# Expert places ranked by token count: capacities of 128, 96 and 64 rows, and the last ten experts two at a time in the array

## The chip, the cores and the metric

The kernel runs on one core of one Trainium2 chip. The metric is the device time of one execution in microseconds, as the median over the runs shown. All data is float32.

## The reference

One step of a single-layer decoder over 1088 tokens (1024 of a prompt, 64 of eight samples). RMSNorm and one input projection feed an RWKV-7 head group and a dilated-attention head group; their outputs are projected and added to h. Then comes the mixture of experts, which this case is about, then a gated per-layer embedding and a last RMSNorm.

```python
x = RMSNorm(h)                                    # 1088 x 1024
lg = x @ rgw + rgb;  gsel = argmax(lg)            # one of 4 groups
le_sel = (x @ rew + reb)[gsel]                    # 8 experts of that group
top_p, top_i = top_k(softmax(le_sel), 2)          # two experts per token
gate[token, expert] = softmax(lg)[gsel] * top_p / sum(top_p)
hg = silu(x @ ewg[e]) * (x @ ewu[e])              # 32 experts, 1024 -> 256
h += sum_e (hg * gate[:, e]) @ ewd[e]             # 256 -> 1024
```

There are 32 experts and 1088 x 2 = 2176 (token, expert) choices.

## The kernel before, in words

`build` runs five stages one after another: `inputs`, `rwkv`, `attention`, `feed_forward`, `finish`. Between the last two stands `later_passes`, which is skipped when no expert has more than CAP = 128 tokens (L2171: `most > CAP`).

`feed_forward` first projects the mixer outputs, normalises, and computes router logits. VectorE picks each token's experts (L1935 to L1962). TensorE counts (`rank`, L1717). VectorE works out each token's place in its expert and a one-hot of the places (L1965 to L1968), and TensorE multiplies that with the token numbers (`find`, L1723), so that bank 7 holds, for every expert, the list of its tokens. VectorE casts it to `idx` (L1973), which releases GpSimd's gathers and SyncE's load of expert 3.

Then comes the loop over the 32 experts in their own order, each with 128 rows whatever its count. For expert e:

- GpSimd gathers 128 token rows of 1024 values (0.5 MB) from HBM into one of three buffers (L1652).
- TensorE turns them (`gather_turn`, L1737: 8 transposes), VectorE copies the result out as `xT` (L2019).
- TensorE computes gate and up (`up`, L1750): for each of 2 matrices, 2 halves of the 256 hidden columns and 8 blocks of the contraction, one matmul with 128x128 *weights* as the stationary operand and 128 tokens as the moving one, 32 in all. A float32 matmul stands in the profile as two records, so 64.
- ScalarE applies silu (L1859), VectorE multiplies by the up half (L2030), giving `hT`.
- TensorE computes the down projection (`down`, L1762): 4 matmuls with `hT` stationary and 512 moving columns, 8 records. ScalarE copies out (L1827) and stores 0.5 MB to `y_rows` (L1830).

TensorE's order is written out by hand (L1794 to L1801): up(e), gather_turn(e+1), down(e-1), then up(e+1). Weights (three DMAs of 1 MB per expert, `load_expert`, L1560 to L1564) go into a ring of NW = 4 slots, slot e % 4. SyncE issues the load of expert e only when down(e-4) is done, since that frees the slot (L1634 to L1636). After down(29) it loads the 4 MB of the embedding gate into slots 0 and 1 (L1639 to L1641).

VectorE also works out, in turns 1 and 2, the row and weight of every token's result (`rows`, L1985), 33 small operations each.

`finish` gathers each token's two result rows (L2209), adds them, normalises, and does the last projection with TensorE (L2271, L2286).

Of the kernel before, what the change touches and what calls it, by code (L numbers as in the profile page):

```python
# [1544 lines left out]
NW, NX = 4, 3  # L1545
WSIZE = 2 * KD * FF + 2 * D
# [19 lines left out]

def feed_forward(nc, g):
# [3 lines left out]
    with ExitStack() as ctx:  # L1571
# [12 lines left out]
        w4, w32, br = w3[:, at + 256:at + 256 + G], w3[:, at + 260:at + 260 + NE], w3[:, at + 292:at + 292 + G + NE]  # L1584

# [6 lines left out]
        gated = g.gated = sb("gated", [128, 2, 2, 2 * CAP])  # L1592
        sg_, hT = ([gated[:, a, i, :].rearrange("p (f q) -> p f q", f=2) for i in range(2)] for a in range(2))
# [6 lines left out]
        pos, t1, t2, over, mx, pg, dl, rstd, ffn = (g.spare[:, a:a + TT] for a in range(330, 330 + 9 * TT, TT))  # L1600
        m2 = g.spare[:, 420:420 + 2 * TT].rearrange("p (k t) -> p k t", k=2)
# [4 lines left out]
        valid, tokv = sb("valid", [128, TT]), sb("tokv", [128, TT])  # L1606
# [5 lines left out]
        LOADS = ((gain, g.d_ffn_gain), (wr, g.d_wr), (br, g.d_br), (upper, g.d_upper), (iota, g.d_iota), (valid[:, :], g.d_valid),  # L1612
                 (w4, g.d_w4), (w32, g.d_w32), (tokv[:, :], g.d_tokv), (i32t, g.d_i32t), (pad_a, g.d_pad_a))
        with nc.Block() as block:
            @block.sync
            def _(sp):
# [27 lines left out]
            def _(pool):  # L1644
# [4 lines left out]
                for e in range(NE):  # L1649
                    if e >= NX:  # L1650
                        pool.wait_ge(s["x_turned"], e - NX + 1)
                    pool.indirect_dma_start(xg[e % NX], None, g.xn[:, :], bass.IndirectOffsetOnAxis(idx[:, e:e + 1], 0)).then_inc(xg_in[e % NX], 16)  # L1652
# [3 lines left out]
            def _(pe):  # L1656
# [74 lines left out]
                def gather_turn(e):  # L1731
                    pe.wait_ge(xg_in[e % NX], 16 * (e // NX + 1))
                    if e >= 1:
                        pe.wait_ge(s["xev"], e)
                    v = xg[e % NX].rearrange("p (q k) -> p k q", k=KD)
                    for k in range(KD):
                        mm = pe.transpose(bank[4 + k // 4][:, 128 * (k % 4):128 * (k % 4) + 128], v[:, k, :], g.ident[:, :])  # L1737
                    mm.then_inc(s["x_turned"], 1)

                def up(e):  # L1740
                    i = e % NW
                    pe.wait_ge(s["xev"], e + 1)
                    pe.wait_ge(w_in[i], 48 * (e // NW + 1))
                    wg, wu, _ = weights[i]
                    if e >= 2:
                        pe.wait_ge(s["h"], e - 1)
                    for a, w in enumerate((wg, wu)):
                        for f in range(2):
                            for k in range(KD):
                                mm = pe.matmul(bank[6 + e % 2][:, 128 * (2 * a + f):128 * (2 * a + f) + CAP], w[:, k, 128 * f:128 * f + 128],  # L1750
                                               xT[e % 2][:, k, :], start=(k == 0), stop=(k == KD - 1))
                    mm.then_inc(s["up"], 1)

                def down(e):
                    pe.wait_ge(s["h"], e + 1)
                    if e >= 2:
                        pe.wait_ge(s["yev"], e - 1)
# [109 lines left out]
            def _(dve):  # L1867
                def op(ins):
                    dve.drain()
# [674 lines left out]
```

## Time and profile before

| | us |
|---|---|
| median of 3 runs (1776.92 to 1789.27) | 1778.75 |
| the profiled execution's own time | 1779.9 |
| its span, first to last instruction | 1778.1 |
| TensorE busy | 1628.3 (92%) |
| VectorE busy | 672.5 (38%) |
| ScalarE busy | 434.6 (24%) |
| expert loop, first up to end of last down | 1249.6 to 1617.6 |

The span is what the profile shows; the time around it is 1.8 us. PE is TensorE's matmul side, PEld its weight loads, DVE VectorE, ACT ScalarE, POOL GpSimd, SP SyncE; SPq marks instructions of SyncE's queue. PEclk is the granted TensorE clock as a share of 2.4 GHz.

### The profile page before, as it was taken

What the parts mean: (1) busy time and instruction counts of PE and PEld (TensorE: products, weight loads), DVE (VectorE), ACT (ScalarE), POOL (GpSimd) and SP (SyncE); (2) the same over time, 40 slices, a digit from 0 to 9 for tenths busy, and PEclk for the clock granted to TensorE, in tenths of its full rate; (3) what the DMA queues carried; (4) which work ended last, traced back from release to release, by engine and by line L of the source; (5) the groups of instructions that cost most, each with busy time, mean ns of one, the idle gap of its engine ahead of it and who ended that gap; (6) DMA issues with size and microseconds to landing.
All of it is one profiled execution on the core that took longest, in us unless ns stands there. A gap on an engine that the chain in (4) does not pass through costs nothing. (4 is left out here: it accounts for less than half of the span.)

```text
span 1778.1 us, 34951 instructions
## 1 busy us (share of the span) xinstructions
PE 1628.3 (92%) x15296; PEld 1144.4 (64%) x15296; DVE 672.5 (38%) x1631; ACT 434.6 (24%) x891; POOL 55.5 (3%) x57
## 2 busy tenths in 40 slices
PE   7899989989988889998989879999999999995997
PEld 4566775775676656675757654555788888883443
DVE  5365464464364213415151442234411111112564
ACT  4413314214202202304131231112111111111344
POOL 0000000000000000000000000000100000002110
PEclk9898999998997889999999989999999999997999
DMA  5000001000010043403242472004799999976321
GB/s 183 27 27 12 15 17 38 13 16 13 15 41 20 3 195 129 169 27 155 119 179 119 186 276 97 36 36 158 273 368 368 366 371 368 365 297 221 111 83 42
DMA packets 57597, 246.90 MB, mean 139 GB/s; under 512 B 7520, under 2 KB 18016, under 8 KB 47712
## 3 DMA queue, kind: packets, MB, share of 16 engines
q1 hardware_dynamic: 45632, 201.61, 30.3%
q0 software_dynamic: 7200, 26.22, 4.1%
q10 hardware_dynamic: 4608, 16.78, 2.3%
q8 instruction: 123, 2.02, 0.5%
q14 instruction: 34, 0.28, 0.1%
HBM read 210.70 MB, written 33.88 MB: 138 GB/s over the span
## 5 line engine op out<-in xcount | busy, mean ns | idle before, releaser
L438 PE MATMUL bank<-h,w 128*128 128x352 f32 (+1 forms) x576 | 198.6, 495 | 6.4 <-DVE xb L997 6.4
L1750 PEld LDWEIGHTS bank<-cache,we 128*128 128x128 f32 x1536 | 175.1, 192 | 13.7 <-issue 10.5
L1750 PE MATMUL bank<-cache,we 128*128 128x128 f32 x1536 | 175.6, 275 | 2.8 <-DVE cache L2019 2.8
L438 PEld LDWEIGHTS bank<-h,w 128*128 128x128 f32 x576 | 109.7, 198 | 69.6 <-DVE xb L997 7.6
L2019 DVE COPY cache<-bank 128x512 f32<-128x512 f32 x64 | 41.3, 686 | 289.3 <-PE bank L1737 289.3
L1241 PE MATMUL bank<-h,w 128*128 128x352 f32 (+1 forms) x384 | 120.8, 477 | 5.5 <-POOL qd L1226 5.5
L1681 PE MATMUL bank<-cache,mixed 128*128 128x512 f32 x256 | 113.0, 600 | 6.4 <-DMA mixed<-in_pad_a 6.4
L2286 PE MATMUL bank<-we,unT 128*128 128x512 f32 x256 | 114.2, 604 | 1.4 <-DVE unT L2237 1.4
L1241 PEld LDWEIGHTS bank<-h,w 128*128 128x128 f32 x384 | 74.2, 194 | 50.4 <-POOL qd L1226 6.1
L1681 PEld LDWEIGHTS bank<-cache,mixed 128*128 128x128 f32 x256 | 48.7, 193 | 65.5 <-issue 58.9
L2286 PEld LDWEIGHTS bank<-we,unT 128*128 128x128 f32 x256 | 48.9, 194 | 60.4 <-issue 58.6
L1762 PE MATMUL bank<-we,gated 128*128 128x512 f32 x192 | 86.4, 592 | 0.0
L1297 PE MATMUL bank<-ident,score 128*128 128x128 f32 x288 | 45.9, 294 | 26.5 <-ACT score L1416 14.1
L1257 PEld LDWEIGHTS bank<-w,h 128*128 128x128 f32 (+1 forms) x576 | 65.3, 186 | 2.6
L1257 PE MATMUL bank<-w,h 128*128 128x128 f32 (+1 forms) x576 | 66.0, 275 | 0.0
L1444 DVE TENSOR_TENSOR eT<-bank,sin 128x352 f32<-128x352 f32 (+1 forms) x24 | 12.8, 536 | 138.1 <-PE bank L1249 136.7
L1827 ACT ACTIVATE cache<-bank 128x512 f32<-128x512 f32 x64 | 34.7, 594 | 123.5 <-PE bank L1762 123.5
L1297 PEld LDWEIGHTS bank<-ident,score 128*128 128x128 f32 x288 | 32.3, 146 | 50.1 <-ACT score L1416 28.5
L1859 ACT ACTIVATE gated<-bank 128x256 f32<-128x256 f32 x32 | 12.3, 385 | 199.2 <-PE bank L1750 199.2
L1750 PEld LDWEIGHTS bank<-cache 128*128 128x128 f32 x512 | 58.4, 192 | 3.8 <-issue 3.8
L1480 DVE CUSTOM_DVE_ANT_0 score<-bank,count 128x512 f32<-128x512 f32 (+3 forms) x96 | 50.9, 555 | 26.4 <-PE bank L1286 26.4
L1750 PE MATMUL bank<-cache 128*128 128x128 f32 x512 | 58.5, 275 | 0.0
(405 smaller groups left out, 2499.2 us busy)
## 6 DMA issues: line engine op xcount, KB each, us to landing
we<-in_weg SPq DMA_DIRECT2D x24, 1024.0 KB, 5.3
we<-in_weu SPq DMA_DIRECT2D x24, 1024.0 KB, 8.6
we<-in_wed SPq DMA_DIRECT2D x24, 1024.0 KB, 11.2
cache<-in_kcj SPq DMA_DIRECT2D x4, 5120.0 KB, 15.7
cache<-in_vcj SPq DMA_DIRECT2D x4, 5120.0 KB, 15.1
y_rows<-cache ACTq DMA_DIRECT2D x32, 512.0 KB
cache<-in_weg SPq DMA_DIRECT2D x8, 1024.0 KB
cache<-in_weu SPq DMA_DIRECT2D x8, 1024.0 KB
```

The source lines that it names most:

```text
L438: mm = pe.matmul(out[:, 0:w], w3[:, KIND[q], kd, :], g.uT[:, kd, a:a + w], start=(kd == 0), stop=(kd == KD - 1))
L1241: mm = pe.matmul(bank[QK[i][n]][:, 0:w], w3[:, k, i, :], g.uT[:, k, a:a + w], start=(k == 0), stop=(k == KD - 1))
L1257: mm = pe.matmul(bank[2 + n % 2][0:rows, 128 * (t - t0):128 * (t - t0) + 128], g.uT[:, k, 128 * t:128 * t + rows], w3[:, k, 2, :], start=( ...
L1297: mm = pe.transpose(bank[x % 2][:, 128 * (b - b0):128 * (b - b0) + 128], score[:, i % 2, hh, 128 * b:128 * b + 128], g.ident[:, :])
L1444: dve.tensor_tensor(turned[:, a:a + w], bank[QK[i][n]][:, 0:w], sin[:, a:a + w], ALU.mult)
L1480: dve.tensor_tensor_reduce(out=score[:, i % 2, hh, 512 * b:512 * b + w], in0=bank[4 + 2 * hh + (b if i >= 4 else i % 2)][:, 0:w], in1=coun ...
L1681: mm = pe.matmul(bank[2 * part + i][:, :], rows[:, k, 128 * t:128 * t + 128], wo[:, J * part + k, 512 * i:512 * i + 512], start=(k == 0), ...
L1750: mm = pe.matmul(bank[6 + e % 2][:, 128 * (2 * a + f):128 * (2 * a + f) + CAP], w[:, k, 128 * f:128 * f + 128], xT[e % 2][:, k, :], start= ...
L1762: mm = pe.matmul(bank[2 * (e % 2) + c][:, :], hT[e % 2][:, f, :], weights[e % NW][2][:, f, 512 * c:512 * c + 512], start=(f == 0), stop=(f ...
L1827: last = act.activation(yo[:, e % 2, 512 * c:512 * c + 512], bank[2 * (e % 2) + c][:, :], ACT.Copy)
L2019: last = dve.tensor_copy(xT[e % 2][:, 4 * c:4 * c + 4, :].rearrange("p k q -> p (k q)"), bank[4 + c][:, :])
L2286: mm = pe.matmul(bank[4 + 2 * (t % 2) + i][:, :], uT[:, t % 2, k, :], wp[:, k, 512 * i:512 * i + 512], start=(k == 0), stop=(k == KD - 1))
```

## The change

Experts are sorted by their number of tokens, and each gets a *place* in the loop. Places 0 to 3 stay experts 0 to 3, whose weights are loaded before the counts are known. Places 0 to 9 have room for 128 rows, 10 to 21 for 96, 22 to 31 for 64. The last ten places are taken two at a time (a *pair*), so the loop has 27 turns. A pair's 64 + 64 tokens are the *stationary* operand, 64 columns each, in the two column halves of the array, and the weight matrices the moving one with 256 columns. Its result comes out with tokens on the partitions, so after silu and multiplication it is turned (`hidden_turn`).

```diff
+CAPS = [128] * 10 + [96] * 12 + [64] * 10
+BASE = [sum(CAPS[:e]) for e in range(NE)]
+TURNS = [(e,) for e in range(NE) if CAPS[e] > 64]
+TURNS += [(e, e + 1) for e in range(len(TURNS), NE, 2)]
+turn_of = lambda e: next(u for u, places in enumerate(TURNS) if e in places)
```

SyncE's load loop:

```diff
                 sp.wait_ge(s["p_done"], TT)
-                sp.wait_ge(s["idx"], 1)
+                sp.wait_ge(s["ordered"], 2)
                 load_expert(sp, g, weights[3], 3, w_in[3])
                 for e in range(NW, NE):
-                    sp.wait_ge(s["down"], e - NW + 1)
-                    load_expert(sp, g, weights[e % NW], e, w_in[e % NW])
-                sp.wait_ge(s["down"], NE - 2)
+                    which = sp.value_load(order[0:1, e:e + 1], min_val=0, max_val=NE - 1)
+                    sp.wait_ge(s["down"], turn_of(e - NW) + 1)
+                    load_chosen(sp, g, weights[e % NW], which, w_in[e % NW])
+                sp.wait_ge(s["down"], turn_of(NE - 3) + 1)
```

GpSimd's gathers, one per place:

```diff
+                    for i, e in enumerate(places):
+                        pool.indirect_dma_start(xg[u % NX][64 * i:64 * i + CAPS[e], :], None, g.xn[:, :],
+                                                bass.IndirectOffsetOnAxis(idx[0:CAPS[e], e:e + 1], 0)).then_inc(xg_in[u % NX], 16)
```

TensorE (`gather_turn` turns the `rows_in(u)` rows that a turn has instead of 128):

```diff
+                def up(u):
+                    pe.wait_ge(s["xev"], u + 1)
+                    for e in TURNS[u]:
+                        pe.wait_ge(w_in[e % NW], 48 * (e // NW + 1))
+                    if len(TURNS[u]) == 2:
+                        for a in range(2):
+                            for k in range(KD):
+                                for i, e in enumerate(TURNS[u]):
+                                    mm = pe.matmul(bank[6 + u % 2][64 * i:64 * i + 64, 256 * a:256 * a + 256], xT[u % 2][:, k, 64 * i:64 * i + 64],
+                                                   weights[e % NW][a][:, k, :], start=(k == 0), stop=(k == KD - 1))
+                    else:
...
+                                    mm = pe.matmul(bank[6 + u % 2][:, 128 * (2 * a + f):128 * (2 * a + f) + CAPS[e]], weights[e % NW][a][:, k, 128 * f:128 * f + 128],
+                                                   xT[u % 2][:, k, 0:CAPS[e]], start=(k == 0), stop=(k == KD - 1))
+                def hidden_turn(u):
+                    pe.wait_ge(s["gated"], pairs_to(u))
+                    for f in range(2):
+                        mm = pe.transpose(bank[6 + u % 2][:, 128 * f:128 * f + 128], sg_rows[u % 2][:, 128 * f:128 * f + 128], g.ident[:, :])
                 def down(u):
...
+                            for i, e in enumerate(TURNS[u]):
+                                mm = pe.matmul(bank[2 * (u % 2) + c][64 * i:64 * i + CAPS[e], :], hT[u % 2][:, f, 64 * i:64 * i + CAPS[e]],
+                                               weights[e % NW][2][:, f, 512 * c:512 * c + 512], start=(f == 0), stop=(f == 1))
...
+                for u in range(NU):
+                    up(u)
+                    if u + 1 < NU:
+                        gather_turn(u + 1)
+                    if u >= 1:
+                        down(u - 1)
+                    if len(TURNS[u]) == 2:
+                        hidden_turn(u)
+                down(NU - 1)
```

VectorE between the one-hot of the places and the loop. The products with `pairs` and `each` have 32 x 32 values, and so have the sums over them; ahead of the copy to `order` one operation on 32 values is left out, ahead of the copy to `g.most` nine, which give each expert's capacity and first row:

```diff
-                op(dve.tensor_reduce(most, bank[5][:, 0:NE], AX.X, ALU.max))
-                dve.tensor_copy(g.most[:, :], most)
+                op(dve.tensor_copy(counts, bank[5][:, 0:NE]))
+                op(dve.scalar_tensor_tensor(out=key, in0=counts, scalar=float(NE), in1=fixed, op0=ALU.mult, op1=ALU.add))
+                op(dve.tensor_tensor(chosen, pairs(key), each(key), ALU.is_gt))
+                op(dve.tensor_reduce(spot, chosen, AX.X, ALU.add))
+                op(dve.tensor_tensor(chosen, pairs(spot), each(i32t), ALU.is_equal))
                 dve.wait_ge(s["found"], 1)
-                dve.tensor_copy(idx[:, :], bank[7][:, 0:NE]).then_inc(s["idx"], 1)
+                op(dve.tensor_tensor(turns, pairs(bank[7][:, 0:NE]), chosen, ALU.mult))
+                op(dve.tensor_reduce(key, turns, AX.X, ALU.add))
+                dve.tensor_copy(idx[:, :], key).then_inc(s["idx"], 1)
+                dve.tensor_tensor(turns, pairs(i32t), chosen, ALU.mult)
+                op(dve.tensor_reduce(key, turns, AX.X, ALU.add))
...
+                dve.tensor_copy(order[:, :], key).then_inc(s["ordered"], 1)
...
+                dve.tensor_copy(g.most[:, :], most).then_inc(s["ordered"], 1)
```

VectorE in the loop, where `rows` becomes two parts: `first_rows` has 4 operations on 288 values and 7 on 9 values, `later_rows` 4 on 288 and 41 on 9. And the condition of `later_passes`, where `most` is now the largest excess of a count over its expert's capacity:

```diff
-                    if e in (1, 2):
-                        rows(e - 1)
+                    if u in (1, 2):
+                        first_rows(u - 1)
+                    if u in (3, 4):
+                        later_rows(u - 3)
...
-        with nc.If(most > CAP):
+        with nc.If(most > 0):
```

`load_chosen` is `load_expert` with the expert's number taken from a register. A pair's silu and product work on 128 partitions x 256 as before; the product goes back over `sg_rows`, and VectorE copies the turned result to `hT`. ScalarE stores only the rows a turn has (0.5, 0.375 or 0.5 MB).

## Rows read from the trace of the kernel before

**Rows 1.** One stretch of the expert loop: busy time per engine (count), PEclk, DMA share, GB/s
```profile
1440.00:1480.00 40.00, 40.00 (x272) 32.59 (x272) 6.06 (x12) 5.50 (x11) 3.58 (x4) 1.00 0.97 366
```

**Rows 2.** Timeline of one turn of the loop: start, duration, engine, line, operation
```profile
1404.11 1.05 PE L1737 MATMUL bank<-ident,w 128*128 128x128 f32 x8
...
1405.00 3.60 PE L1762 MATMUL bank<-we,gated 128*128 128x512 f32 x8
...
1408.44 7.31 PE L1750 MATMUL bank<-cache 128*128 128x128 f32 x64
...
1409.68 0.43 SPq L1564 DMA_DIRECT2D we<-in_wed  x1
...
1415.58 1.05 PE L1737 MATMUL bank<-ident,w 128*128 128x128 f32 x8
```

**Rows 3.** Waits of SyncE's queue, 1200 to 1640 us: total, times, longest
```profile
SPq L1562 <- PE bank L1762: 290.0, 28, 23.1
```

**Rows 4.** DMA issues of the loop, 1280 to 1560 us: KB each, us to landing
```profile
we<-in_wed SPq DMA_DIRECT2D x19, 1024.0 KB, 10.9
```

**Rows 5.** Timeline: matmuls with 96 and 32 moving columns, and with 64-column weights
```profile
1210.49 1.92 PE L1698 MATMUL bank<-we,cache 128*128 128x96 f32 x16
...
1236.87 4.10 PE L1728 MATMUL bank<-gated,cache 128*128 128x32 f32 x36
...
1759.05 7.09 PE L2292 MATMUL bank<-we,unT 128*64 128x512 f32 x32
```

**Rows 6.** Expert weights loaded alone: the issue, and GB/s in 40 slices of 1216-1240
```profile
1217.66 0.33 SPq L1562 DMA_DIRECT2D we<-in_weg  x1
...
GB/s 0 0 0 0 137 55 410 437 437 437 423 423 437 369 396 430 444 355 41 20 20 0 0 0 0 0 0 0 0 0 0 0 0 0 0 0 0 0 0 0
```

**Rows 7.** DMA issues of the attention, 560 to 900 us: two loads issued together
```profile
cache<-in_vcj SPq DMA_DIRECT2D x2, 5120.0 KB, 15.6
...
w<-in_wqkv SPq DMA_DIRECT2D x2, 1536.0 KB, 18.8
```

**Rows 8.** TensorE after a wait: stretches, and weight loads after 14 us of little work
```profile
1617.60:1635.90 18.30, 0.00 (x0) 0.00 (x0) 3.64 (x5) 3.70 (x6) 6.60 (x6) 0.59 0.66 231
...
1640.00:1645.00 5.00, 5.00 (x7) 1.94 (x6) 2.77 (x5) 1.35 (x3) 2.85 (x2) 0.53 0.31 88
...
1064.41 0.50 PEld L1681 LDWEIGHTS bank<-cache,mixed 128*128 128x128 f32 x2 [6.51 <-DMA mixed<-in_pad_a]
...
1067.14 0.34 PEld L1681 LDWEIGHTS bank<-cache,mixed 128*128 128x128 f32 x1 [0.52 <-issue]
...
1067.95 0.19 PEld L1681 LDWEIGHTS bank<-cache,mixed 128*128 128x128 f32 x1 [0.47 <-issue]
```

**Rows 9.** Timeline from the routing to the first turn of the loop
```profile
1235.61 1.36 DVE L1968 TENSOR_TENSOR cache<-we,mixed 128x1152 f32<-128x1152 f32 x1
...
1241.01 0.19 DVE L1973 CAST idx<-bank 128x32 int32<-128x32 f32 x1 [3.52 <-PE bank L1728]
...
1247.04 1.16 PE L1737 MATMUL bank<-ident,w 128*128 128x128 f32 x8 [0.69 <-DMA w<-xn_rows,idx]
...
1249.59 7.41 PE L1750 MATMUL bank<-cache,we 128*128 128x128 f32 x64 [1.38 <-DVE cache L2019]
```

**Rows 10.** Timeline of VectorE: the first and last operation of rows(0), the next eviction
```profile
1269.13 0.45 DVE L1988 TENSOR_TENSOR v<-oh,mixed 128x288 f32<-128x288 f32 x1
...
1277.81 0.17 DVE L2012 CAST first_row<-mixed 128x9 int32<-128x9 f32 x1
...
1279.07 1.29 DVE L2019 COPY cache<-bank 128x512 f32<-128x512 f32 x2 [1.08 <-PE bank L1737]
```

**Rows 11.** Timeline at the end of the loop
```profile
1603.56 4.17 SPq L1641 DMA_DIRECT2D we<-in_pgate  x8
...
1613.95 3.60 PE L1762 MATMUL bank<-we,gated 128*128 128x512 f32 x8
...
1623.41 0.94 POOL L2209 DMA_INDIRECT cache<-y_rows,first_row  x1 [56.51 <-issue]
```

More of the change, by code:

```diff
@@ L1545 @@
 NW, NX = 4, 3
+CAPS = [128] * 10 + [96] * 12 + [64] * 10
+BASE = [sum(CAPS[:e]) for e in range(NE)]
+TURNS = [(e,) for e in range(NE) if CAPS[e] > 64]
+TURNS += [(e, e + 1) for e in range(len(TURNS), NE, 2)]
+NU = len(TURNS)
+turn_of = lambda e: next(u for u, places in enumerate(TURNS) if e in places)
+rows_in = lambda u: sum(CAPS[e] for e in TURNS[u])
+pairs_to = lambda u: sum(len(places) == 2 for places in TURNS[:u + 1])
+gathers_to = lambda u: sum(len(TURNS[n]) for n in range(u % NX, u + 1, NX))
 WSIZE = 2 * KD * FF + 2 * D
@@ L1758, in down @@
+                def hidden_turn(u):
+                    pe.wait_ge(s["gated"], pairs_to(u))
+                    for f in range(2):
+                        mm = pe.transpose(bank[6 + u % 2][:, 128 * f:128 * f + 128], sg_rows[u % 2][:, 128 * f:128 * f + 128], g.ident[:, :])
+                    mm.then_inc(s["h_turned"], 1)
+                def down(u):
+                    pe.wait_ge(s["h"], u + 1)
+                    if u >= 2:
+                        pe.wait_ge(s["yev"], u - 1)
                     else:
@@ L1969, in _ @@
                 op(dve.memset(g.now[:, :], 1.0))
-                op(dve.tensor_reduce(most, bank[5][:, 0:NE], AX.X, ALU.max))
-                dve.tensor_copy(g.most[:, :], most)
-                dve.wait_ge(s["found"], 1)
-                dve.tensor_copy(idx[:, :], bank[7][:, 0:NE]).then_inc(s["idx"], 1)
+                pairs = lambda x: x.unsqueeze(1).broadcast_to([128, NE, NE])
+                each = lambda x: x.unsqueeze(2).broadcast_to([128, NE, NE])
+                turns = place[0].rearrange("p t q -> p (t q)")[:, 0:NE * NE].rearrange("p (r e) -> p r e", r=NE)
@@ new lines, in _ @@
+                op(dve.tensor_scalar(key, spot, float(NE - CAPS.count(64)), 32.0, ALU.is_lt, ALU.mult))
+                op(dve.scalar_tensor_tensor(out=cap, in0=key, scalar=64.0, in1=cap, op0=ALU.add, op1=ALU.add))
+                dve.tensor_scalar(key, spot, float(NE - CAPS.count(64)), 32.0, ALU.min, ALU.mult)
+                dve.tensor_scalar(counted, spot, float(CAPS.count(128)), 32.0, ALU.min, ALU.mult)
+                dve.drain()
+                op(dve.scalar_tensor_tensor(out=spot, in0=spot, scalar=64.0, in1=key, op0=ALU.mult, op1=ALU.add))
@@ L1992, in rows, with later_rows @@
+                def later_rows(k):
+                    p, eid = position[:, k, :], pos
+                    of_expert(k, t1, cap)
+                    op(dve.tensor_tensor(over, p, t1, ALU.is_ge))
+                    op(dve.tensor_tensor(t1, t1, over, ALU.mult))
+                    op(dve.tensor_tensor(p, p, t1, ALU.subtract))
+                    for m in range(1, PASSES - 1):
                         op(dve.tensor_scalar(t1, p, float(CAP * m), None, ALU.is_ge))
                         op(dve.tensor_tensor(over, over, t1, ALU.add))
-                    n = PASSES * NE
@@ L2510, in build @@
             g.now = sm("now", [128, 1])
-            g.row, g.turn = sm("row", [128, 2, TT]), sm("turn", [128, 2, TT])
+            g.row, g.turn = (g.spare[:, a:a + 2 * TT].rearrange("p (k t) -> p k t", k=2) for a in (538, 556))
             g.weight, g.first_row = sm("weight", [128, 2, TT]), sm("first_row", [128, 2, TT], i32)
```

204 lines of the change are left out of this document (111 added, 93 removed).

## Prediction

> **What bounds the kernel now.** I read the windows of the loop first, then one turn in the timeline, then who waits for whom. In the loop TensorE is busy in 40.00 of 40 us at full clock, while the DMA engines are busy 97% of the time and move 366 GB/s [rows 1]. Two resources look full, so the next view has to say which one ends a turn. A turn runs from one gather_turn to the next, 1404.11 to 1415.58 = 11.47 us [rows 2]: 8 transposes 1.0, down 3.4, up 7.1. No wait stands between these pieces. SyncE's queue, on the other hand, waits for TensorE's down in 28 turns, 290.0 us in all [rows 3]. So TensorE sets the pace, and a load is issued only when a down has freed a slot. The third DMA of a load is issued at 1409.68, 1.05 us after the first, and lands 10.9 us after its own issue [rows 2, 4]. A whole load thus takes 12.0 us from its first issue, a little more than a turn, and four slots give it about two turns before its weights are used. The transfers are hidden, but by little: 3.15 MB of weights, 0.52 MB gathered and 0.52 MB stored per turn are 4.19 MB in 11.47 us, 365 GB/s, which is what rows 1 show.
>
> **96 moving columns instead of 128.** Sixteen records with 96 moving columns take 1.92 us and 36 with 32 columns take 4.10 us [rows 5]. Without the last record's tail (0.28) that is 0.110 and 0.109 us each, and up's 64 records take 7.31 [rows 2], 0.112 each. A quarter of the columns buys nothing: the 128-column weight load sets this pace. The twelve places of 96 rows save at most 0.002 x 64 x 12 = 1.5 us; I take 0. Their down is unchanged (512 moving columns), their transposes have the same weights. Smaller gathers and stores only relieve the DMA, which is hidden there.
>
> **A pair's turn on TensorE.** 32 records with 64-column weights in alternating column halves and 512 moving columns take 7.09 us, 0.21 us each after a tail of 0.4 [rows 5]; with 128-column weights a record of 512 takes 3.4 / 8 = 0.43 [rows 2]. So two halves do run beside each other. Up of a pair is 2 matrices x 8 blocks x 2 experts = 32 matmuls = 64 records with 256 moving columns, half of 0.21, so 64 x 0.107 + 0.2 = 7.1 us. Down is 16 records of 0.215 = 3.5. Transposes 1.0, hidden_turn 0.3. The tensor work of two experts falls from 22.9 to about 11.9 us. For five pairs that is 55 us of TensorE. The question is whether the weights keep up.
>
> **The weights of a pair.** They don't. A pair fills two of four slots, and down of pair i, which frees them, stands in TensorE's program behind up of pair i+1. That up waits for both of its own loads. So up(P1) runs, then down(P0), and only then are the loads of P2 issued; TensorE has nothing left but hidden_turn, and waits for the whole of two loads. Meanwhile, through an up, the DMA queue is empty. The two resources, which overlapped before, take turns.
>
> How long do two loads take? One load alone is issued at 1217.66, streams from 1219.6 at about 430 GB/s and has ended by about 1226.8 [rows 6]: 9.2 us, of which 7.2 stream. Twice the streaming gives 9.2 + 7.2 = 16.4, plus 1.2 for the 0.52 MB store beside it = 17.6. The other bound: 5.24 + 1.57 MB issued together land 18.8 us after the second issue, 19.2 after the first [rows 7]; 6.29 MB at that rate, with 2 us lead, take 17.9, with the store 19.2. I take 18.5, near the middle, because addresses now come from a register, whose issue the trace doesn't show (0 to 1 us). Value_load itself waits ahead of the slot's release, or behind DMAs in flight, so I give it nothing.
>
> After such a wait TensorE starts slow. Its clock was 0.59 over a wait of 18.3 us and still 0.53 at 1640 to 1645 [rows 8], half of 2.4 GHz. In dense work the slow stretch is shorter: from 1064.41 the weight loads come 0.86 us apart and from 1067.95 on 0.43 [rows 8], so 3.5 us of slow work, which costs 1.75. The sparse case has 9 us of slow work, 4.4 at most. I take 2.0 per pair after the first, as its up is dense; bounds 0 and 4.4.
>
> Now the sum, with t = 0 at the start of up(21), the last single turn. The weights of place 23 are issued at 0 and land by about 11.5 to 12, just when up(P0) can start: 11.5. Up 7.1, gather_turn 1.0, down(21) 3.4: 23.0. Only now is the second load of P1 issued, alone: 9.2 + 1.2 = 10.4, so up(P1) starts at 33.4. Slow start 2.0, up 7.1, turn 1.0, down(P0) 3.5: 47.0, and + 18.5 = 65.5 is the start of up(P2). Each further pair takes 18.5 + 2.0 + 7.1 + 1.0 + 3.5 = 32.1: up(P3) at 97.6, up(P4) at 129.7. Then 9.1 for that up, down(P3) 3.5, hidden_turn and the copy of its result 0.9, down(P4) 3.5: 146.7. Changes between 128- and 64-column work cost some 0.2 per pair, 1.0. End at 147.7. Before, the same stretch is ten turns and the last one's up and two downs, 114.7 + 7.1 + 3.4 + 3.6 = 128.8; the last down ends at 1617.55 [rows 11]. The tail is 18.9 us longer.
>
> **The ordering on VectorE.** 1152 values take 1.36 us [rows 9], so each of the products and sums over 1024 takes 1.3 with its drain, a small one 0.25. From 1236.97: memset, copy and key 0.6, three large 3.9, which ends at 1241.5 and covers the wait for `found` (1241.0); two large and the cast 2.85: idx at 1244.35 instead of 1241.20 [rows 9], +3.15. The gathered rows reach TensorE 5.84 us after idx [rows 9], now at 1250.2. Behind idx VectorE has two large and 13 small operations and the gates (2.1): free at 1251.9, about when the transposes, slow after a 3.8 us pause, are done. Up(0) starts at 1253.8 instead of 1249.59, +4.2, and its slow start adds about 1.8: **+6.0**. If the clock stays up, +4.2 or less. Queued behind SyncE's wait for `ordered` is the load of place 3, 3.5 us later, needed only three turns on.
>
> **later_rows.** rows(k) takes 33 operations from 1269.13 to 1278.0, and VectorE was then idle for 1.1 us until the next eviction [rows 10]. later_rows has 4 x 0.53 + 41 x 0.246 = 12.2 us, 3.3 more. It ends 2.3 us after the transposes are done; down (3.4) hides most, 0.4 is left. The second one starts late by that and ends 2.9 after up could start: together **+3.3**. first_rows (3.9) is hidden in both turns.
>
> **The end.** The 4 MB for `finish` were issued at 1603.56, 14 us before the loop's end; now they follow down(P3), 4 to 5 us before it. The first gathers of finish start 5.9 us after the last down [rows 11] and share the DMA with the rest: **+1.5**, between 0 and 4.
>
> Sum: 6.0 + 3.3 + 18.9 + 1.5 = +29.7. On the profiled time 1779.9 that is 1809.6; the median is 1.15 lower, so **1808.5**, 1.7% slower. A change under 1% can hardly be told from none.
>
> **Rivals.**
> *B, transfers and TensorE still overlap.* If the slots came free early enough, the DMA alone would bound the pairs: 6.29 + 1.05 MB at 366 GB/s = 20.0 us per pair. Up(P4) would start at 11.5 + 80 = 91.5 and the loop end at 107.5, 21.3 earlier than before; with 10.8 for the other terms, 1768. It decides if loads of P2 begin before down(P0). The semaphore in SyncE's queue speaks against it.
> *B2, TensorE alone bounds the pairs*, 11.9 us each: 33 us earlier still, 1736. It needs 6.29 MB in 11.9 us = 530 GB/s; the fastest slices show 444 [rows 6].
> *C, fewer moving columns do count.* A quarter off up's 7.15 us in twelve turns is 21 us: 1787. The rows with 32 columns speak against it. The Trainium skill, TensorE: Matmul & The Clock Gate, section Back-to-back issue gap, gives a spacing by moving columns alone for an isolated matmul; by that rule the 96-row turns would gain, and the trace has no sign of it.
> *D, the halves run one after the other* at 256 columns: up +7.1, down +3.5, all five on the chain, +53: 1861. Rows 5 speak against it. The Trainium skill, same page, section Packing small matmuls, says that weight loads overlap with running matmuls only where the row group differs, and here both halves have the same rows; by that rule up would have its loads exposed. The 7.09 us of rows 5 contradict it.
> *E, a place overflows* and the later passes run: eight passes of at least 32 x 11.5, over 2,900 us more. The reference's own choices on its inputs give 103 tokens at most, 81 from place 10 on and 62 from place 22 on, so two rows are spare.
>
> **How the numbers follow.** Forecast 0.75, B 0.08, B2 0.04, C 0.07, D 0.04, E 0.02. The forecast's own range: without any slow clock and late VectorE -13, loads at 17.6 -3; slow stretches of 4.4 +10, loads at 20 +5, finish +2.5: 1792 to 1826. To leave out no more than 2 in 10 I reach down to C: 1786 to 1826. Faster by over 1% is B2 and the lower part of B, 0.07. Within 1% is the rest of B, C, and the forecast's lower end, 0.18. Slower by over 1%: 0.75.
>
> **What would show it.** A timeline in which from the second pair on TensorE idles 18 us ahead of every pair's up with "DMA we" as the releaser; SyncE's DMA share falling to half in the last 130 us; up of a pair 7.1 us (9 with the slow start); single turns still 11.47, also those of 96 rows; idx at about 1244.4; two short waits for VectorE in turns 5 and 6. Wrong would be a turn of 96 rows under 11 us, pairs every 20 us, or a pair's up of 14 us.

## The result, and the profile after

| | before | after |
|---|---|---|
| median, range, us | 1779.56 (1776.92 to 1789.27, 4 runs) | 1832.73 (1824.95 to 1841.63, 4 runs) |
| profiled execution: time, span, us | 1779.9, 1778.1 | 1833.85, 1832.0 |
| mean granted clock of TensorE | 0.953 | 0.925 |

The ratio after to before is 1.0286, 95% interval 1.0257 to 1.0316: 2.9% slower, where 1.7% was forecast. 1832.73 lies above the range (1786 to 1826); one of the four executions, 1824.95, lies in it. The two spans differ by 53.9 us, and the starts of TensorE's groups in the two traces divide them:

| stretch | forecast | measured |
|---|---|---|
| up to the routing's rank matmul (code that the change doesn't touch) | 0 | +3.1 |
| rank matmul to the start of up(0) | +4.2 | +4.1 |
| up(0), slow clock | +1.8 | +2.4 |
| up(2) to up(7), later_rows | +3.3 | +5.15 |
| up(7) to up(21), mostly 96-row turns | 0 | -0.4 |
| up(21) to the end of the last down (the tail) | +18.9 | +34.9 |
| last down to the first transposes of finish | +1.5 | +4.5 |
| from there to the end | 0 | +0.1 |

The first row is drift. In other executions of the changed code, and of the experiments', that rank matmul stands between 1229.3 and 1240.1 us with nothing ahead of it changed. Below I therefore compare, beside the ratios, the stretch from this matmul to the end of the span: 547.7 us before, 598.5 after. It is one profiled execution of each kernel.

The page after, its slices (45.8 us each): TensorE's busy tenths, its clock, the DMA, GB/s.

```profile
PE   7889989999988898989989879998999996434997
PEclk9898998998996899999999989998999997766999
...
DMA  5000000000000044242240750044989995565321
GB/s 177 26 26 13 25 16 25 16 25 14 23 24 13 8 184 174 116 174 116 110 179 26 283 223 35 35 161 141 365 321 351 344 349 207 198 249 196 103 92 41
```

From the 34th slice (1511 us) TensorE falls to 6, 4, 3 and 4 tenths, its clock to 0.7 and 0.6, and the DMA, nearly full until then, to half. The windows say it more closely (columns as in [rows 1]):

```profile
1440.00:1480.00 40.00, 40.00 (x272) 31.79 (x272) 5.13 (x12) 4.55 (x10) 4.51 (x5) 1.00 0.96 356
...
1560.00:1600.00 40.00, 16.04 (x98) 8.69 (x94) 2.46 (x5) 2.56 (x5) 0.00 (x0) 0.74 0.53 199
1600.00:1640.00 40.00, 14.66 (x90) 8.37 (x90) 2.04 (x4) 1.47 (x3) 0.00 (x0) 0.67 0.58 228
```

The first is the window of [rows 1] again: 96-row turns, TensorE full, and the GB/s only a little lower because less is gathered and stored. In the pair turns both resources, which overlapped, are about half busy. TensorE's waits, 1240 to 1690 us, name what it waits for:

```profile
PE bank L1783 <- DMA we<-in_wed: 75.4, 5, 19.6
...
PE bank L1790 <- DVE cache L2115: 5.7, 4, 2.4
PE bank L1769 <- DMA w<-xn_rows,idx: 4.0, 1, 4.0
```

Before, there was no wait for `in_wed` in the loop. Now each of the five pairs' ups waits, 75.4 us together. The timeline of one 96-row up and of one pair:

```profile
1434.48 7.28 PE L1790 MATMUL bank<-cache,we 128*128 128x96 f32 x64
...
1561.09 0.34 SPq L1582 DMA_DIRECT2D cache<-in_weg  x1
...
1563.14 0.34 SPq L1582 DMA_DIRECT2D we<-in_weg  x1
...
1580.84 0.66 PE L1783 MATMUL bank<-cache 128*64 128x256 f32 x1 [19.56 <-DMA we<-in_wed]
...
1590.50 1.16 PE L1769 MATMUL bank<-ident,w 128*128 128x128 f32 x8
```

Up with 96 moving columns takes 7.28 us, with 128 it took 7.31 [rows 2]; a 96-row turn is 11.43 us (1434.48 to the next up at 1445.91). Down(P0) ends at 1560.9, SyncE issues P2's two loads at 1561.09 and 1563.14, and up(P2) starts at 1580.84, after 19.56 us of idling; it takes 9.66 us, its first record 0.66 instead of 0.38 at full clock. Pairs follow each other every 34.3 us.

The other terms: the routing to the first up (as [rows 9] for the kernel before), the up behind the second late copy, and the end (as [rows 11]).

```profile
1233.53 0.75 PE L1750 MATMUL bank<-gated,we 128*128 128x288 f32 x2 [2.48 <-DVE gated L2015]
...
1247.72 0.18 DVE L2037 CAST idx<-we 128x32 int32<-128x32 f32 x1
...
1253.43 1.97 PE L1769 MATMUL bank<-ident,w 128*128 128x128 f32 x8 [3.99 <-DMA w<-xn_rows,idx]
...
1256.78 9.84 PE L1790 MATMUL bank<-cache,we 128*128 128x128 f32 x64 [1.38 <-DVE cache L2115]
...
1329.73 9.04 PE L1790 MATMUL bank<-cache 128*128 128x128 f32 x64 [2.36 <-DVE cache L2115]
...
1662.31 4.03 SPq L1670 DMA_DIRECT2D we<-in_pgate  x8
...
1667.98 0.33 ACTq L1881 DMA_DIRECT2D y_rows<-cache  x1
...
1676.92 0.94 POOL L2315 DMA_INDIRECT cache<-y_rows,first_row  x1 [144.55 <-issue]
```

Idx comes 14.4 us behind the rank matmul. Before, that matmul stood at 1230.45 and idx at 1241.01 [rows 9], 10.7 with the cast's own time. The transposes wait 3.99 us for the gathered rows instead of 0.69, and the up behind them is slow. At the end, finish's first gather follows the last store's issue by 8.9 us; before it was 4.7 (1618.70 to 1623.41 [rows 11]).

### The profile page after: what moved, and what is told of

Its sections match the earlier page's. It is cut to its first block and busy times, and to the rows that moved or that the text cites. A ratio compares the mean times of both kernels' runs of the same rounds, so it can differ in the third digit from the quotient of the medians.

```text
span 1832.0 us, 34516 instructions
## 1 busy us (share of the span) xinstructions
PE 1593.4 (87%) x14946; PEld 1094.8 (60%) x14946; DVE 683.5 (37%) x1684; ACT 426.4 (23%) x876; POOL 54.8 (3%) x57
## 5 line engine op out<-in xcount | busy, mean ns | idle before, releaser
L2115 DVE COPY cache<-bank 128x512 f32<-128x512 f32 (+1 forms) x54 | 31.6, 626 | 293.2 <-PE bank L1769 292.9
L1790 PEld LDWEIGHTS bank<-cache,we 128*128 128x128 f32 x1088 | 126.3, 195 | 11.7 <-issue 6.9
L1790 PE MATMUL bank<-cache,we 128*128 128x96 f32 (+1 forms) x1088 | 126.7, 278 | 3.4 <-DVE cache L2115 3.4
L1810 PE MATMUL bank<-we,gated 128*96 128x512 f32 (+2 forms) x192 | 79.5, 594 | 0.0
L1783 PE MATMUL bank<-we,cache 128*64 128x256 f32 x224 | 48.9, 480 | 32.2 <-DMA we<-in_wed 32.2
L1783 PE MATMUL bank<-cache 128*64 128x256 f32 x96 | 29.3, 481 | 43.2 <-DMA we<-in_wed 43.2
L1878 ACT ACTIVATE cache<-bank 128x512 f32<-128x512 f32 (+1 forms) x54 | 29.2, 592 | 106.8 <-PE bank L1810 106.8
L1783 PEld LDWEIGHTS bank<-we,cache 128*64 128x64 f32 x224 | 29.0, 176 | 38.8 <-issue 36.5
## 6 DMA issues: line engine op xcount, KB each, us to landing
we<-in_wed SPq DMA_DIRECT2D x24, 1024.0 KB, 11.9
```

What stands on the lines that cost most here:

```text
L1783: mm = pe.matmul(bank[6 + u % 2][64 * i:64 * i + 64, 256 * a:256 * a + 256], xT[u % 2][:, k, 64 * i:64 * i + 64], weights[e % NW][a][:, k, ...
L1790: mm = pe.matmul(bank[6 + u % 2][:, 128 * (2 * a + f):128 * (2 * a + f) + CAPS[e]], weights[e % NW][a][:, k, 128 * f:128 * f + 128], xT[u ...
L1810: mm = pe.matmul(bank[2 * (u % 2) + c][64 * i:64 * i + CAPS[e], :], hT[u % 2][:, f, 64 * i:64 * i + CAPS[e]], weights[e % NW][2][:, f, 512 ...
L1878: last = act.activation(yo[0:n, u % 2, 512 * c:512 * c + 512], bank[2 * (u % 2) + c][0:n, :], ACT.Copy)
L2115: last = dve.tensor_copy(xT[u % 2][:, 4 * c:4 * c + 4, 0:n], bank[4 + c][:, :].rearrange("p (k q) -> p k q", k=4)[:, :, 0:n])
```

## The experiments

All edits are on the changed kernel. Times are medians; "before" is the kernel before in the same session; "behind rank" is the stretch defined above. The kernel before moved by up to 7 us between sessions, so times of different rows are compared by their ratios or behind rank. e4, e5 and e10 leave work out and e9 loads the weights of other experts; these four serve for timing alone, with two executions each.

| run | us | before | ratio (95%) | behind rank |
|---|---|---|---|---|
| after | 1832.73 | 1779.56 | 1.0286 (1.0257 to 1.0316) | 598.5 |
| e1_all_single | 1797.92 | 1783.95 | 1.0087 (1.0058 to 1.0115) | 562.4 |
| e2_down_first | 1769.62 | 1783.95 | 0.9936 (0.9889 to 0.9983) | 535.0 |
| e3_keep_busy | 1826.52 | 1783.95 | 1.0245 (1.0228 to 1.0262) | 588.7 |
| e4_gather_128 | 1830.9 | 1783.95 | 1.0268 (1.0235 to 1.0301) | 592.9 |
| e5_half_loads | 1809.37 | 1784.93 | 1.0136 (1.0105 to 1.0168) | 574.5 |
| e6_later_spread | 1830.35 | 1784.93 | 1.0253 (1.0226 to 1.0280) | 595.7 |
| e7_gate_after_store | 1838.9 | 1778.03 | 1.0341 (1.0309 to 1.0372) | 603.2 |
| e8_order_and_spread | 1771.53 | 1784.93 | 0.9922 (0.9899 to 0.9945) | 531.1 |
| e9_fixed_addresses | 1831.65 | 1784.93 | 1.0261 (1.0229 to 1.0293) | 596.5 |
| e10_no_pair_gathers | 1829.72 | 1781.97 | 1.0257 (1.0175 to 1.0339) | 588.4 |

### e1_all_single: the ranking without the pairs

```diff
-TURNS = [(e,) for e in range(NE) if CAPS[e] > 64]
-TURNS += [(e, e + 1) for e in range(len(TURNS), NE, 2)]
+TURNS = [(e,) for e in range(NE)]
```

> The ranking and the three capacities stay, but all 32 places are turns of their own, the last ten with 64 moving columns. Theory: the pairs cost what the forecast missed, and the rest of the change costs about 16 us over the kernel before (4.1 and 2.4 at the start, 5.2 for later_rows, 4 at the end of which 3 vanish here because the 4 MB of the embedding gate are issued a whole turn ahead again). So a single turn of 64 rows takes 11.4 us like one of 128, and the time is 1779.6 + 12 to 13 = about 1792 us. Rival: it is the ordering and the smaller transfers that made the change slow; then this kernel stays above 1815.

Measured: 0.87% over before, 14.7 us behind rank, some 2 us more than expected. The waits for `in_wed` are gone. Ranking and later_rows cost about what they cost in the changed kernel: up(0) starts 23.1 us behind rank and lasts 10.22, up(2) to up(7) take 62.5. The 64-row turns take 11.7 to 11.9 us and make the stretch from up(21) to the end of the last down 4.0 us longer than before:

```profile
1558.11 7.36 PE L1789 MATMUL bank<-cache 128*128 128x64 f32 x64
...
1566.42 3.65 PE L1809 MATMUL bank<-we,gated 128*64 128x512 f32 x8
```

Half the moving columns leave up at 7.36, and half the weight columns leave down at 3.65: fewer moving columns alone, or fewer weight columns alone, win nothing. The turn even grows by 0.3 to 0.4 us. So the pairing, with the later issue of the 4 MB that it brings, makes the difference between 1.0087 and 1.0286, 2.0%.

### e2_down_first: the down that frees the slots ahead of the pair's up

```diff
 for u in range(NU):
+    if len(TURNS[u]) == 2:
+        down(u - 1)
     up(u)
     if u + 1 < NU:
         gather_turn(u + 1)
-    if u >= 1:
+    if u >= 1 and len(TURNS[u]) == 1:
         down(u - 1)
```

> From the first pair on, down of the turn before stands ahead of up of the turn. The same work, other order. Theory (slots): the wait for weights comes from the slots being freed behind the next up; freed ahead of it, loads run beside the up, and a pair takes 20 to 21 us (6.8 MB at 367 GB/s is 18.6, and there is a lead of 1 to 2) instead of 34.3, the first pairs gain some 8 us as well: about 50 us less, 1782 us. TensorE then waits some 7 us per pair, and mostly starts slow still. Rival (rate): the transfers' rate bounds the stretch in any order; then the pairs stay at 34 us and the time at 1832.

Measured: 1769.62 us, 3.4% under the changed kernel (0.9936 / 1.0286) and 0.6% under the kernel before, more than the 50 us expected: 63.5 behind rank. The stretch of four pairs, and TensorE's waits in 1240 to 1690:

```profile
1519.00:1593.00 74.00, 55.68 (x360) 32.51 (x360) 8.16 (x16) 5.43 (x12) 1.79 (x2) 0.91 0.96 373
```
```profile
PE bank L1783 <- DMA we<-in_wed: 14.2, 5, 4.8
PE bank L1798 <- DVE gated L2128: 7.8, 5, 1.7
```

No byte is saved, no matmul left out. The DMA share goes from 0.53 to 0.96, the waits for weights from 75.4 to 14.2 us, and pairs come every 18.6 us. Its new order has a price too: hidden_turn now waits 1.7 us for VectorE in four of the five pairs, and two of the downs behind it run slow, 5.35 us instead of 3.65. The long wait is the order's. That the DMA bounds the pairs once the order is right is read from its share of 0.96 and the waits that remain; no run varies the bytes in this order.

### e3_keep_busy: TensorE works through the waits

```diff
-for e in TURNS[u]:
-    pe.wait_ge(w_in[e % NW], 48 * (e // NW + 1))
 if u >= 2:
     pe.wait_ge(s["h"], u - 1)
+if len(TURNS[u]) == 2:
+    for _ in range({22: 4, 23: 14}.get(u, 22)):
+        pe.matmul(bank[6 + u % 2][:, :], g.ident[:, :], g.h[:, 0, 0:512], start=True, stop=True)
+for e in TURNS[u]:
+    pe.wait_ge(w_in[e % NW], 48 * (e // NW + 1))
```

> Ahead of the wait for a pair's weights TensorE multiplies rows of h with the identity into the bank that up overwrites next: 4 matmuls for the first pair, 14 for the second, 22 for the other three, 0.86 us each at full clock. Nothing else changes. Theory: the low clock after a wait costs 2.4 to 2.8 us per pair; with it gone up takes 7.1 us instead of 9.6 to 9.9 and five pairs give 10 to 13 us back: about 1820 us. Rival: the clock costs nothing, since the loads set the pace; then no change from 1832.

Measured: 0.4% below the changed kernel, with intervals that overlap a little; behind rank it is 9.8 us less, where 10 to 13 were expected. In the trace the dummy work stands where the idling was. From the second pair on the granted clock stays at 1.00 (0.74 in this window of the changed kernel), and pairs come every 31.4 us with ups of 7.13:

```profile
1560.00:1600.00 40.00, 39.61 (x158) 19.57 (x155) 2.47 (x5) 2.55 (x5) 0.00 (x0) 1.00 0.60 227
```
```profile
1561.03 19.05 PE L1778 MATMUL bank<-h,ident 128*128 128x512 f32 x44
...
1580.46 0.40 PE L1786 MATMUL bank<-cache 128*64 128x256 f32 x1 [0.39 <-DMA we<-in_wed]
```

So the slow start costs 2.5 to 2.8 us per pair (the changed kernel's ups of 9.62 to 9.93 against 7.13), where I had taken 2.0; the pairs follow each other 2.9 sooner, because the weights are there 0.3 earlier as well. The first pair isn't helped: its four dummy matmuls are over before the weights are there, it waits another 4.0 us, starts 19.0 us behind up(21) and takes 8.60. The 7.13 us also settle rival D. The plainest pair of rows on it is down: in e1 eight records with 64 columns take 3.65 us, one half working alone, and in a pair of the changed kernel sixteen records in the two halves take the same 3.65, so the halves run beside each other:

```profile
1591.58 3.65 PE L1810 MATMUL bank<-we,gated 128*64 128x512 f32 x16
```

### e5_half_loads: one load per pair

```diff
 for e in range(NW, NE):
+    if e >= 26 and e % 2:
+        continue
...
 for e in TURNS[u]:
-    pe.wait_ge(w_in[e % NW], 48 * (e // NW + 1))
+    if e < 26 or e % 2 == 0:
+        pe.wait_ge(w_in[e % NW], 48 * (e // NW + 1))
```

> From place 26 on only the even place of a pair has its weights loaded and waited for; the odd place computes with what its slot held before, so the arithmetic on TensorE is the same and one transfer per pair (P2, P3, P4) is left out. Theory (the pair's wait is the transfer of two loads that starts only after the down): the wait ahead of up falls from 19.6 us to about 10.5 (one load: 9.2 alone, 1.2 for the store beside it), a pair's turn from 34.3 to about 25, three times 9.1 = 27 us less, 1805 us. Rival (a fixed cost of each pair, such as reading the load's address from a register, or the semaphore between the engines, is a large part of the wait): the wait stays above 15 us and the total falls by less than 15 us.

Measured: 1809.37, 1.5% below the changed kernel, 24.0 us less behind rank where 27 were expected. The three waits are 11.61, 11.87 and 11.62 us, not 10.5:

```profile
1600.49 1.12 PE L1786 MATMUL bank<-we,cache 128*64 128x256 f32 x4 [11.87 <-issue]
```

Half the bytes take 7.8 us off a wait of 19.5: the wait is the transfer, and only about 3.9 us of it don't depend on the bytes (an estimate from these two waits). 3.15 MB in 7.8 us is 404 GB/s on average, not the 430 at which I had let it stream, and a single load takes 12.0 to 12.2 us from the down's end, where 10.4 was forecast.

### e9_fixed_addresses: loads without a register

```diff
-    which = sp.value_load(order[0:1, e:e + 1], min_val=0, max_val=NE - 1)
     sp.wait_ge(s["down"], turn_of(e - NW) + 1)
-    load_chosen(sp, g, weights[e % NW], which, w_in[e % NW])
+    load_expert(sp, g, weights[e % NW], e, w_in[e % NW])
```

> Places 4 to 31 load the weights of the expert with the place's own number, from addresses fixed in the program, and no value is read from the order; ranking, gathers and turns stay, so the outputs are those of wrongly paired weights. Theory (a load that is issued with an address from a register is issued later and lands later: the load of place 23 took 15.5 us and made the first pair wait 4.3 us; the second load of a pair is issued 2.05 us after the first): the first pair's wait falls below 2 us and each later pair's from 19.6 to about 18.5, 5 to 6 us in all, about 1828 us. Rival (the addresses cost nothing, the two small gathers and the store share the DMA with the loads): the waits stay 4.3 and 19.6 within 0.5 us.

Measured: no difference (1.0261 beside 1.0286, the intervals overlap); the waits of P2 to P4 are 19.4, 19.2 and 19.1, and the first pair's is 6.6, longer than with the register and not shorter. So addresses from a register cost 0.1 to 0.4 us per pair, and they don't explain the late first pair.

### e4_gather_128 and e10_no_pair_gathers: why the first pair starts late

Up(P0) was forecast 11.5 us behind up(21). It came 16.0 us after it in the changed kernel, and 17.8 to 19.0 after it in e3, e5, e6, e7 and e9, whose gathers and loads there are the same. So the profiled execution of the changed kernel was the luckiest of six, and a difference under 3 us between two traces says little here. e4 gathers once per pair, 128 rows (the count of gathers that TensorE waits for is changed with it):

```diff
-for i, e in enumerate(places):
-    pool.indirect_dma_start(xg[u % NX][64 * i:64 * i + CAPS[e], :], None, g.xn[:, :],
-                            bass.IndirectOffsetOnAxis(idx[0:CAPS[e], e:e + 1], 0)).then_inc(xg_in[u % NX], 16)
+e = places[0]
+pool.indirect_dma_start(xg[u % NX], None, g.xn[:, :], bass.IndirectOffsetOnAxis(idx[:, e:e + 1], 0)).then_inc(xg_in[u % NX], 16)
```

> Every turn gathers 128 rows with one gather of its (first) place's list, as the kernel before did; a pair's second half gets rows 64 to 127 of the first place's list, so the second place of a pair is left out of the computation. Question: why the load of place 23 landed 15.5 us after its issue, not 12. Theory (a gather costs the same DMA time for 64, 96 or 128 rows, and a pair has two): in the turns of 96 rows nothing changes, although a third more is gathered (the third DMA of a load still lands about 11.8 us after its issue), and the wait ahead of the first pair falls from 4.3 us to 1 to 2. Rival (bytes): loads land later than now in the turns of 96 rows, by 3 to 4% of a turn, and the wait ahead of the first pair stays.

e10 gathers nothing for pairs (again with the count):

```diff
-for i, e in enumerate(places):
+for i, e in enumerate(places if len(places) == 1 else ()):
```

> The ten gathers of the pairs are left out, and their turns compute with rows that an earlier gather left; loads, stores and TensorE's work are unchanged. Theory (the gathers run three turns ahead, so eight of the ten stand in the last single turns, where the DMA is already full, and each costs it over 1 us whatever its rows; this backlog makes the load of place 23 late): up(P0), which started 16.0 to 19.4 us after up(21) in the runs with these gathers and 14.5 with half of them, starts 11.5 to 12.5 us after it, that is with a wait under 1 us and without a slow start; the later pairs' waits stay near 19.5. About 7 us less in all, 1826 us. Rival (the load is late because the load after it is issued 11.5 us behind it and shares the DMA, whatever is gathered): up(P0) still starts over 15 us after up(21).

Measured: with ten gathers 16.0 to 19.0 us (six traces), with five (e4) 14.5, with none (e10) 12.1 (one trace each). e4's wait of 2.9 us is above the 1 to 2 expected; in its 96-row turns nothing changed (11.43 us), though a third more is gathered. Windows of the last single turns, first the changed kernel, then e10:

```profile
1480.00:1500.00 20.00, 20.00 (x154) 17.48 (x153) 1.48 (x4) 2.82 (x6) 1.78 (x2) 1.00 0.98 332
```
```profile
1480.00:1500.00 20.00, 20.00 (x145) 16.59 (x143) 1.45 (x4) 2.49 (x5) 0.00 (x0) 1.00 0.83 300
...
1517.08 0.40 PE L1783 MATMUL bank<-cache 128*64 128x256 f32 x1 [0.48 <-DMA we<-in_wed]
```

With the gathers the DMA is full (0.98) while it moves only 332 GB/s, less than the 366 of [rows 1]; without them it has air (0.83), the load of place 23 lands in time, and up(P0) runs without a slow start (7.12 us). The gathers run three turns ahead, so the pairs' gathers fall on the last single turns, which carry a full load of weights each. Eight gathers stand there where single turns would have had four, each at 1.1 to 1.2 us of the whole DMA (below), ahead of or beside the first pair's weights. The bytes alone seem not to be it: e4 gathers as many for a pair as two gathers do, the DMA moves 362 GB/s at a share of 0.95 there (1480 to 1520), and its up(P0) is earlier than in any of the six traces, though by 1.5 us only. The later waits stay at 19.3 to 19.5, as expected. Behind rank e10 is 10 us below the changed kernel, where 7 were expected; its two executions leave the ratio too wide to tell.

### e6_later_spread: later_rows over four turns

later_rows becomes a list of its 90 operations, issued from index 23 * (u - 3) on.

```diff
-if u in (3, 4):
-    later_rows(u - 3)
+if u in (3, 4, 5, 6):
+    for f in steps[(u - 3) * 23:(u - 2) * 23]:
+        f()
```

> The same 90 VectorE operations of later_rows, but 23 of them in each of turns 3 to 6 instead of 45 in each of turns 3 and 4. Theory (the 5.15 us lost between up(2) and up(7) are VectorE's, which is late with the copies of the transposes in two turns, and a slow start after the second): 23 operations are about 6 us, less than the 12 of rows(k) that a turn already hides, so up(2) to up(7) falls from 62.5 to 57.3 us and the total by 5, to about 1828 us; no wait for the copies over 0.3 us is left. Rival (the turns are late because of the narrower gathers and the transfers, not VectorE): up(2) to up(7) stays above 61 us.

Measured in the trace: up(2) starts at 1281.69, up(7) at 1339.02, 57.33 us, as before the change, and no wait for the copies is left there. The 5.15 us were VectorE's. The ratio falls only by 0.3%, with overlapping intervals, and behind rank 2.8 of the 5 us expected are left, since in this trace the first pair waited 6.6 us, 2.3 more; the total is inconclusive, the stretch isn't.

### e7_gate_after_store: the 4 MB after the last store

```diff
-sp.wait_ge(s["down"], turn_of(NE - 3) + 1)
+sp.wait_ge(s["down"], NU)
+sp.wait_ge(s["stored0"], 16 * -(-NU // 2))
```

> SyncE issues the 4 MB of in_pgate only when the last down is done and the stores of the even turns (the last one's among them) have landed. Theory (the last store takes 8.4 us because these 4 MB, issued 5 us earlier, fill the DMA; that makes the first gathers of finish 4 us late): the store lands about 4 to 5 us after its issue, as it did where the 4 MB had been moved before, finish starts 4 us earlier and the total falls by about 4 to 1829 us; the 4 MB need about 12 us from then and are in before finish multiplies by them. Rival (the store is slow by itself, or the 4 MB are now the late ones): the start of finish stays 10 us behind the last store's issue, or TensorE waits for wp, and the total is the same or more.

A miss: 1.0341, not 0.2% less but some 0.5% more, and 4.7 us more behind rank.

```profile
1669.93 3.97 SPq L1671 DMA_DIRECT2D we<-in_pgate  x8
1675.39 0.33 SPq L2303 DMA_DIRECT2D cache<-in_final_gain  x1
1675.95 0.95 POOL L2316 DMA_INDIRECT cache<-y_rows,first_row  x1 [143.23 <-issue]
```

The store did become fast: issued at 1667.26, it had landed by 1669.93, after 2.7 us instead of 8.4. But SyncE now issues eight DMAs ahead of the block's end, which takes until 1675.39, and the other engines wait for that end; GpSimd's first gather comes 8.7 us behind the store, hardly earlier than 8.9. Then the 4 MB share the DMA with finish's gathers, and finish's first transposes come 27.6 us after the last down instead of 22.9. The 4 MB cost wherever the tail's order has left no room for them. In e2, where they were issued 19 us before the last down's end, the store landed within 4.1 us and this stretch was 17.9 (18.4 before).

### e8_order_and_spread: both edits together

The edits of e2 and e6 together.

> Both edits at once: down of the turn before stands ahead of a pair's up in TensorE's program, and later_rows is spread over four turns. Theory (independent costs, one in the tail, one in turns 3 to 6): the gain of the first (63 us against the changed kernel in the same session's clock) and 5 us more: about 1764 to 1765 us, 0.8 to 1.2% below the kernel before, up(2) to up(7) 57.3 us and pairs every 18 to 19 us. Rival (the DMA is full once the tail runs at 96% of it, and earlier turns only bring forward work that then waits for loads): the total stays at the 1769.6 us of the first edit alone.

Measured: 1771.53 us, ratio 0.9922 (0.9899 to 0.9945), 0.8% below the kernel before and 3.5% below the changed one. Up(2) to up(7) takes 57.33 us, and the stretch behind rank is 531.1 against 535.0 in e2, where up(2) to up(7) took 60.85; so in the traces the gains add. The median doesn't show it: the 1764 to 1765 us expected were missed, and between e2 and e8 no difference can be told.

## Why the prediction was wrong in size, point by point

**What bounds the kernel, 96 columns.** Right. The 96-row turns take 11.43 us against 11.47; rival C is out, and e1 adds that 64 columns gain nothing either.

**A pair's turn on TensorE.** Right: up 7.12 to 7.13 us at full clock (e2, e3, e10) against 7.1, down 3.65 against 3.5. Rival D is out. The row on which this stood, the halves of [rows 5], was read rightly: in e3 a pair's up takes 7.13 us, two records every 0.22, though both halves use the same rows. The Trainium skill, TensorE: Matmul & The Clock Gate, section Packing small matmuls, would expose the weight loads here, as the row group doesn't differ; the trace decides against that rule.

**The weights of a pair.** The mechanism was right: from the second pair on TensorE idles ahead of every up for "DMA we", and e2 and e5 show both halves of it, the order and the transfer. The size was wrong, and this is the failed step, the term "The tail is 18.9 us longer", which measured 34.9. Its parts, in the order of the sum:

| step | forecast | measured | cause |
|---|---|---|---|
| up(21) to up(P0) | 11.5 | 16.0 | "The weights of place 23 ... land by about 11.5 to 12": the DMA is full of the pairs' gathers (e10, in part e4) |
| to up(P1) | 21.9 | 27.3 | up(P0) slow after its own 4.3 us wait (+2.8); one load takes 12.9 from the down's end, not 10.4 (+2.5) |
| to up(P2), up(P3), up(P4) | 32.1 each | 34.5, 34.4, 33.9 | two loads 19.6 to 20.0 from the down's end, not 18.5; slow start 2.5 to 2.8, not 2.0 |
| to the end | 18.0 | 17.7 | |

4.5 + 5.4 + 6.5 - 0.3 is 16.1 us, what the tail misses (34.9 against 18.9, within rounding). The three later steps were inside the bounds of the range (loads at 20, slow stretches of 4.4) and only off the chosen values. What was outside any bound was the first pair. I had let its load land as in a single turn and given the gathers nothing, because "smaller gathers and stores only relieve the DMA": but a pair gathers as many bytes as a turn did before, in two gathers, and two cost the DMA about 2.3 us where one of 128 rows costs 1.3 (below). The same step made up(P0) slow, which I had excluded ("per pair after the first"). e10 shows that the gathers make the first pair late; why the same program is late by 4.5 us in one trace and 7.5 in another stays open.

**The ordering.** Right: +4.1 (4.2) and +2.4 (1.8). Two small errors met: idx came 0.5 us later than forecast, the gathered rows 0.3 sooner behind it. VectorE was done with the gates at 1255.02 and copied at 1255.43, so the gather set the time, as forecast.

**later_rows.** +5.15 instead of +3.3. The two delays were forecast as 0.4 and 2.9 and came as 0.8 and 2.6 (waits of 0.62 and 2.36 for the copies), which is right, and so is where they come (turns 5 and 6). Left out was that after the second the up runs 9.04 us, 1.7 more: a slow start behind a wait of 2.4 us. (In e2 the same wait brought none, and later_rows cost 3.5.) I had counted slow starts only after long waits.

**The end.** +4.5, above the bound of 4. I had the 4 MB beside finish's gathers, but not beside the last store, for whose landing everything waits (8.4 us instead of 4.4).

**The rivals.** B was the road not taken: with the slots free early, pairs come every 18.6 us (e2; I had worked out 20.0), and e2's ratio puts the total at B's 1768. That it fits so well is luck: pairs are faster than in B, but the first one starts 19.5 us behind up(21) and not 11.5. What decided was that the slots come free early enough, which B named as its condition; it needed the other place of down in TensorE's program. B2 and C did not occur; no later pass ran.

**The range.** Its upper end added 17.5 us for slow stretches, loads and finish, but nothing for the first pair, up(0) or later_rows. Four terms (up(0), later_rows, the tail, the end) were all short, by 0.6, 1.9, 16.0 and 3.0 us, and in the profiled execution 3 us of drift ahead of the changed code came on top. The first pair alone, 4.5 us late and 2.8 slow, is more than the 6.7 by which the median left the range.

## What to carry to other kernels

When two units of work share one turn, their buffers are freed together and late. Look at which instruction frees them, and where it stands in the program relative to the one that waits; moving one call was worth 63.5 us here (598.5 to 535.0) and turned a loss of 2.9% into a gain of 0.6%. Where a queue is already 97% busy, price a new arrangement by the number of its transfers as well as by their bytes, and in every stretch into which prefetching moves them, not where they are used. Behind every new wait of TensorE, also one of 2 to 4 us, put a slow start of up to 3 us into the upper end of the range.

## What the runs showed of the hardware that was not expected

- **A gather's DMA time hardly falls with its rows, and falls least where the DMA is full.** The packets of GpSimd's queue took 11.5% of the 16 engines' time before (1280 to 1560 us, 13.1 MB in 25 gathers of 128 rows): 32.2 / 25 = 1.29 us of all 16 engines per gather. In the changed kernel it was 11.6% of 80 us for 2.94 MB in 96-row gathers (1400 to 1480), 7.5 of them, 1.24 us each, and 27.6% of 16.5 us for 1.02 MB (1503 to 1519.5), four 64-row gathers, 1.1 to 1.2 us each. In e1, where the DMA's share is 0.86, seven 64-row gathers took 7.3% of 90 us (1500 to 1590), 0.94 each. So a quarter fewer rows save nearly nothing, and half the rows a tenth in the full stretch and a quarter in the other.
- **How much a wait slows the next up does not follow from its length.** All pair ups of all traces behind waits of 2.9 us and more took 1.35 to 2.9 us over the 7.13. Behind 4.3 us it was 2.8 in the changed kernel, behind 4.4 only 1.35 in e2, and behind 11.6 and 11.9 in e5 it was 2.9 and 1.4. Behind 2.4 us up(P2) in e2 lost 1.7, and the single up(6) took 9.04, 1.7 more, in every trace with the two-turn later_rows but e2's (7.41). Behind 2.0 and 0.5 us (7.13) nothing was lost. When a short wait brings the clock down stays open.
- **A change between weights of 64 and of 128 columns isn't free.** In e1, down with 64-column weights has the same eight records and takes 3.65 us (3.60), and the turn with two such changes is 0.3 to 0.4 us longer. The Trainium skill, TensorEngine Tiling (Array Packing), section Key Properties, says that changing the tiling mode drains TensorE. The longer turn (11.7 to 11.9 us against 11.47) fits that, but no run shows the drain by itself.
- **A second load queued behind the first adds 7.8 us** (e5), 404 GB/s on average over its 3.15 MB, while the same weights loaded alone streamed at about 430 [rows 6].
